# A hybrid transformer block in split fp32r: pair differences split by VectorE, attention weights as neighbour differences, and an earlier split of the first head

## The reference

```
h += 1/2 SwiGLU(RMSNorm(h));  h += StickBreaking(RMSNorm(h));  h += 1/2 SwiGLU(RMSNorm(h))
out = RMSNorm(h)[frames]
```

```
A[t,s] = sigmoid(z_ts) * prod_{s<j<t} (1 - sigmoid(z_tj)),   s < t,   z = q k / sqrt(128)
```

## Time and profile before

| | us |
|---|---|
| median of 3 runs | 2092.15 |
| profiled execution, and its span | 2091.31, 2089.4 |
| PE busy | 1978.4 (95%) |
| PE weight loads busy | 1795.3 (86%) |
| VectorE busy | 1115.4 (53%) |
| POOL busy | 986.9 (47%) |
| ScalarE busy | 684.7 (33%) |

### The profile page before, as it was taken

How to read it: one execution, slowest core, us unless ns; L and a number is a source line. 1 busy time by engine, 2 the same in 40 slices (tenths; PEclk the granted TensorE clock), 3 DMA queues, 4 the chain that set the end, 5 groups by cost and what they waited for, 6 DMA issues and landing times.

```text
span 2089.4 us, 35300 instructions
## 1 busy us (share of the span) xinstructions
PE 1978.4 (95%) x12868; PEld 1795.3 (86%) x12868; DVE 1115.4 (53%) x1587; ACT 684.7 (33%) x1227; POOL 986.9 (47%) x646
## 2 busy tenths in 40 slices
PE   7899999999999997999989999979999999899998
PEld 6899999999999987999978887767777777788886
DVE  5755554544555558333378870275444444454445
ACT  5322222222121233222289981242222222221112
POOL 4654545445444424444477762344454454543340
PEclk9999999999999998999999999989999999999999
DMA  3122222222323201333322112012222222233222
GB/s 123 49 77 87 66 86 71 80 91 103 122 81 102 80 21 51 111 97 106 102 83 71 61 51 61 21 30 66 85 66 84 84 72 85 86 132 115 80 91 81
DMA packets 165366, 167.74 MB, mean 80 GB/s; under 512 B 7984, under 2 KB 130864, under 8 KB 165312
## 3 DMA queue, kind: packets, MB, share of 16 engines
q1 hardware_dynamic: 165312, 166.99, 25.0%
HBM read 126.74 MB, written 40.22 MB: 80 GB/s over the span
## 4 chain that ended last, share of the span: by engine, by line
PE 46%; issue 27%; POOL 16%; ACT 5%; DVE 4%; DMA 1%; POOLq 0%; ACTq 0%; DVEq 0%; SPq 0%
PE psum L1366 15%; PE psum L1367 14%; PE psum L1368 14%; POOL arena L555 13%; PE psum L1393 2%; POOL arena L573 2%; ACT scratch L974 1%; ACT arena L939 1%; DVE scratch L1269 1%; DVE arena L1086 1%; DMA scratch<-w_out_dram 1%; ACT psum L976 1%; DVE psum L1059 0%; PE psum L1586 0%; DMA scratch<-w_o_dram 0%
## 5 line engine op out<-in xcount | busy, mean ns | idle before, releaser
L1366 PE MATMUL psum<-arena 128*128 128x260 f32 (+3 forms) x4028 | 1290.5, 320 | 73.9 <-issue 30.1
L1368 PE MATMUL psum<-arena 128*128 128x260 f32 (+3 forms) x4028 | 1268.9, 315 | 0.0
L1367 PE MATMUL psum<-arena 128*128 128x260 f32 (+3 forms) x4028 | 1267.4, 315 | 0.0
L1366 PEld LDWEIGHTS psum<-arena 128*128 128x128 f32 x4028 | 764.3, 190 | 142.7 <-issue 48.5
L1368 PEld LDWEIGHTS psum<-arena 128*128 128x128 f32 x4028 | 763.1, 189 | 47.1
L1367 PEld LDWEIGHTS psum<-arena 128*128 128x128 f32 x4028 | 763.3, 190 | 46.8 <-issue 3.6
L555 POOL TENSOR_TENSOR arena<-scratch,arena 128x512 fp32r<-128x512 f32 x365 | 509.1, 1417 | 551.7 <-ACT arena L754 551.7
L754 ACT ACTIVATE arena<-scratch 128x512 fp32r<-128x512 f32 x371 | 212.0, 622 | 492.8 <-DMA scratch<-w_in_dram 255.8
L1123 DVE SCALAR_TENSOR_TENSOR h<-psum,h 128x260 f32<-128x260 f32 (+1 forms) x496 | 249.7, 504 | 210.7 <-PE psum L1368 210.5
L1135 DVE TENSOR_TENSOR scratch<-scratch,psum 128x520 f32<-128x520 f32 (+1 forms) x265 | 182.6, 689 | 328.7 <-PE psum L1368 313.5
L1138 DVE TENSOR_TENSOR scratch<-scratch 128x512 f32<-128x512 f32 x200 | 235.6, 1178 | 220.6 <-POOL arena L555 196.3
(11 more groups left out here) (80 smaller groups left out, 1053.0 us busy)
## 6 DMA issues: line engine op xcount, KB each, us to landing
scratch<-w_in_dram SPq DMA_DIRECT2D x88, 512.0 KB, 4.9
scratch<-w_out_dram SPq DMA_DIRECT2D x22, 1024.0 KB, 4.9
qkv<-scratch SPq DMA_DIRECT2D x48, 260.0 KB, 2.1
scratch<-w_qkv_dram SPq DMA_DIRECT2D x24, 512.0 KB, 4.5
scratch<-qkv SPq DMA_DIRECT2D x24, 512.0 KB, 3.7
hidden<-scratch SPq DMA_DIRECT2D x44, 260.0 KB, 2.1
scratch<-hidden SPq DMA_DIRECT2D x11, 1040.0 KB, 4.9
hidden<-scratch SPq DMA_DIRECT2D x44, 256.0 KB, 2.1
```

The costliest lines, as they stand in the source:

```text
L1366: nc.tensor.matmul(dst, wh, xh, start=start, stop=False, skip_group_check=True)
L1367: nc.tensor.matmul(dst, wh, xl, start=False, stop=False, skip_group_check=True)
L1368: return nc.tensor.matmul(dst, wl, xh, start=False, stop=stop, skip_group_check=True)
```

## The change

1. **Homes.** B21 moves from xy and its three neighbours into the region of v1, beside B12 and T3, and v7 shares its region with v3 and no longer with v1. So `copy_x(0)` no longer waits for p_up 2, ScalarE's high parts of T3 wait for the six plain products that read v7, and its high parts of T2 wait for T4.
2. **Order.** The low parts of T1 (v2) go from POOL to VectorE. VectorE makes T1, T3, the first plain_up, the low parts of T1 and T3, and only then T2, T4 and the second plain_up. ScalarE does copy_x(0) before the high parts of T3. In FFN2 the rows of B21 are made after the last add of the output projection and their high parts after the last root.
3. **Attention.** One sigmoid of -z in place in PSUM replaces L974 and L976. POOL subtracts the row's neighbour. At the first step of each block (8 of 14) an extra one-column subtraction clears the row's first entry; at the others POOL also waits for its own previous step. The scan of a last step is one column longer.
4. **First head.** ScalarE's wait for the last QKV unit asks for its third product and no longer for its seventh; POOL splits k and q before it clears the rows.

The diff, cut:

```
-REGION_OF = ((0, 1, 2, 3, 4, 5, 6, 1), (4, 6, 0, 2, 5, 1, 3, 6), (0, 1, 3, 4, 2, 5, 6, 1))
+REGION_OF = ((0, 1, 2, 3, 4, 5, 6, 3), (4, 6, 0, 2, 5, 1, 3, 2), (0, 1, 3, 4, 2, 5, 6, 4))
-LO_BY_DVE = ((4, 6, 3, 1, 5), (6, 3, 1, 5), (6, 3, 1, 5))
-LO_BY_POOL = ((0, 7, 2), (0, 4, 7, 2), (0, 4, 7, 2))
+LO_BY_DVE = ((4, 6, 2, 3, 1, 5), (6, 2, 3, 1, 5), (6, 2, 3, 1, 5))
+LO_BY_POOL = ((0, 7), (0, 4, 7), (0, 4, 7))
...
-            if name == "B21":
-                return flat(n, (xy, c22, u0, scratch[:, 7752:])[k][:, 0:HALF[n]])
-            v, low = {"B12": (3, 1), "T3": (3, 1), "B22": (5, 0), "T2": (5, 0), "T4": (5, 1)}[name]
+            v, low = {"B21": (1, 0), "B12": (1, 1), "T3": (1, 1), "B22": (5, 0), "T2": (5, 0), "T4": (5, 1)}[name]
...
                     pool.wait_ge(left, S * hd + s + 1)
-                    nc.gpsimd.tensor_tensor(row, beta[s % 3][:, 0:n], row, ALU.mult).then_inc(weights, 1)
+                    if first_step(s):
+                        key = row[:, 0:1]
+                        nc.gpsimd.tensor_tensor(key, key, key, ALU.subtract)
+                        row, behind = row[:, 1:], behind[:, 1:]
+                    else:
+                        pool.wait_ge(weights, S * hd + s)
+                    nc.gpsimd.tensor_tensor(row, row, behind, ALU.subtract).then_inc(weights, 1)
...
+            for part_of in (("k", 0), ("k", 1), ("q", 0), ("q", 1)):
+                split(*part_of, 0, 0)
             pool.wait_ge(ffns[QKV]["w_lo"], PRODUCTS * UNITS[QKV])
             nc.gpsimd.memset(scratch[:, 0:21 * P], 0.0).then_inc(const_set, 1)
-            for part_of in (("k", 0), ("k", 1), ("q", 0), ("q", 1)):
-                split(*part_of, 0, 0)
...
                     product_over(u, 0)
-                    if isinstance(u, int) and u == 0:
-                        act.wait_ge(s["p_up"], 2)
-                    else:
-                        act.wait_ge(s["c12"], u)
+                    wait(act, s["c12"], u)
...
                     first_weight(1)
-                    split_rows(n, 3)
                     plain_gate(1)
                     first_weight(5)
                     first_weight(3)
+                    copy_x(0)
+                    split_rows(n, 3)
                     split_rows(n, 1)
-                    copy_x(0)
                     split_rows(n, 5)
...
-                    if not (first and before(s) < 0):
-                        act.wait_ge(weights, S * hd + before(s) + 1)
-                    nc.scalar.activation(beta[s % 3][:, 0:n], bank, ACT.Sigmoid, scale=Q_SCALE).then_inc(broken, 1)
-                    act.wait_ge(broken, S * hd + s + 1)
-                    nc.scalar.activation(bank, beta[s % 3][:, 0:n], ACT.Copy, scale=-1.0, bias=1.0).then_inc(kept, 1)
+                    nc.scalar.activation(bank, bank, ACT.Sigmoid, scale=-Q_SCALE).then_inc(kept, 1)
...
-            act.wait_ge(ffns[QKV]["used"], PRODUCTS * UNITS[QKV])
+            act.wait_ge(ffns[QKV]["used"], PRODUCTS * (UNITS[QKV] - 1) + 3)
...
                 combine(n, "T1", "B12", "B11", over_split=0)
                 combine(n, "T3", "B22", "B12", over_split=7)
+                plain_up(0)
+                rows_lo(n, 2)
+
+                dve.wait_ge(ffns[n]["w_lo"], 4)
+                rows_lo(n, 3)
                 combine(n, "T2", "B22", "T1", over_split=6)
                 combine(n, "T4", "B21", "T2")
-
-                dve.wait_ge(norms[n]["un"], STEPS_TO["T4"] + HK)
-                plain_up(0)
-                rows_lo(n, 3)
                 plain_up(1)
                 rows_lo(n, 1)
                 rows_lo(n, 5)
```

More of the change, by code:

```diff
@@ L204, in build @@
         plain_x = plain("plain_x", 6 * 1024, (META_TILE + 1) * D_MODEL)
-        plain_regions = {j: plain(f"plain{j}", 6 * 1024 + (PRODUCTS - 1 - j) * 4160, 4160) for j in range(1, 6)}
+        plain_regions = {j: plain(f"plain{j}", 6 * 1024 + (PRODUCTS - 1 - j) * 4160, 4160) for j in (1, 5, 6)}
         arena = sbuf("arena", [P, 35392], F32R)
@@ L269, in build @@
         rows = [scratch[:, at:at + tiles * P] for at, tiles in zip(ROW_AT, ROW_TILES)]
-        beta = [scratch[:, at:at + cols] for at, cols in zip(BETA_AT, (BANK, 400, 400))]
         raw_v = piece(scratch, 3592, TOKENS)
@@ L746, in norm_halves @@
                     root(c)
-                if n != FFN2:
-                    split_rows(n, 4)
+                split_rows(n, 4)
                 if n == FFN1:
@@ L803, in plain_gate @@
                     act.wait_ge(s["p_used"], 3 + 4 * c)
-                    if n == QKV and c == 1:
-                        act.wait_ge(norms[n]["un"], STEPS_TO["T4"] + HK)
                     out, bank = flat(n, (g0, (g1 if ffn else c22))[c][:, 0:half]), target(n, "ab"[c])
@@ L1083, in rows_lo @@
                 for k in range(HK):
+                    if v == 1:
+                        lo_made(dve, n, 3, k)
                     ins = inputs(n, v)
@@ L1311, in _ @@
                     rows(FFN2, "B11")
-                if n == KT + 5:
-                    rows(FFN2, "B21")
                 add_output(n)
+            rows(FFN2, "B21")
             reciprocal(FFN2, 1)
```

22 lines of the change are left out of this document (9 added, 13 removed).

## The result

The changed kernel takes **2050.56 us** (median of 4 runs, 2046.47 to 2053.36), beside 2091.18 us for the kernel before in the same comparison (2082.39 to 2094.78). The ratio is 0.9826, interval 0.980 to 0.9852. The forecast was 2061 us, its range 2049 to 2076. A repeat in a later comparison gave 2048.72 us beside 2079.31 for the kernel before: the changed kernel's time repeats, while the gain (40.6 us here, 30.6 there) moves with the kernel before. The experiments take that up.

The account below looks back on a forecast made before the run. PE was taken as bound by stops in the first units and before the first score, and by nearly full engines in the attention; 18.0 + 5.1 + 6.8 = 29.9 us off 2091.3 gave 2061 us, range 2049 to 2076.

Parts of the forecast that it names:

- What bounds the first units: Unit 0, three stages: copy_x(0), then the chain to plain_up stops PE; 4.5, 4.5, 4.7 us stops left, gain 18.0 us.
- The stops before were taken as constants: Unit 0: gain is stop before (6.86 us FFN1, 12.33 QKV, 12.51 FFN2) minus stops after, 18.0 us.
- The clock: First units: slow stretch expected behind the second stop as before; no change booked, upper end 5.6 us.
- T1's low parts at nothing: First units: four instructions moved to VectorE, 3.1 us, up to twice that beside POOL, costed at nothing.
- Into the attention: Before the first score: splits end earlier, PE starts near 1043.0 and not 1048.15, gain 5.1 us.
- The attention: Eight heads: ScalarE relieved of 6.3 us a head; 0.85 us a head gained, 6.8 in all, at most 11.0.
- The attention gives nothing: Rival, attention: PE waits for VectorE, as full as before; gain 23.1 us, 2068 us, chance 0.15.
- POOL is starved: First units rival: low parts wait behind VectorE, 4 to 12 us, or T2, T4 slowed, 13; 2073 us, chance 0.15.
- Slower: Rival, attention: POOL's extra instructions at 0.9 us each lengthen heads; 2115 us, break-even 0.69 us each, chance 0.03.
- All of it: Rival, whole kernel: clock doesn't fall and attention gets its 11.0 us; gain 41.7 us, 2050 us, chance 0.12.

Follow-up runs that it names:

- attention-alone kernel: The kernel before with only the change's attention (one sigmoid in place, POOL's subtraction, longer scan), units and entry as before: 2064.97 us, ratio 0.9925.

## Why the prediction came out as it did, step by step

- **What bounds the first units: right.** The copy and the chain to the second plain_up are where it put them. The first stops are 0.74, 0.74 and 0.73 us (0.8 expected), product 3 starts 9.8, 9.4 and 9.7 us behind product 0's end (10.2), and plain_up ends the second stop. The second stops are 3.06, 2.66 and 3.29 us, not 3.7, 3.7 and 3.9: T3's low parts take 2.45 us from start to start in QKV and not the 3.09 of the earlier trace rows, which were taken while POOL was at work on low parts of its own; here POOL was idle (its last one ended at 801.62). Products 4 and 2 take 6.0 us in FFN1 and QKV and not 5.7, and 5.7 in FFN2 and not 5.5. All stops together are 11.2 us against 13.7: 2.5 us of the miss.
- **The stops before were taken as constants: this is the step that was lucky.** The sum took 6.86, 12.33 and 12.51 us as what these stages cost. But each stage has one of two outcomes in a given run, 6.1 to 6.9 and 12.3 to 13.1. Three short ones would have made the gain some 12 us smaller, and the kernel before ranges from 2073.8 to 2094.8 us over all comparisons, where the changed one, whose second stops repeat within 0.1 us, stays within 2046.5 to 2053.4. The time itself fell at the edge of the range: 2050.56 us is 1.6 above its lower end, and the repeat, 2048.72, is below it.
- **The clock: half right, and that by chance.** In FFN1 and QKV it fell behind the second stop as forecast; behind the 3.29 us stop of FFN2 it stayed up, and there the slow stretch that the kernel before paid was spared. FFN2's stops account for 12.51 - 4.02 = 8.5 us of its 10.6. Windows of PE in the changed kernel (length, busy, granted clock), at 1.2 GHz in the first two and at 2.4 in the third:

```profile
77.00:78.00 1.00, 1.00 (x7) 0.50 0.59 181
811.00:812.00 1.00, 1.00 (x7) 0.50 0.78 258
1366.00:1367.00 1.00, 1.00 (x6) 1.00 0.71 225
```

  The forecast booked no change in any stage, with 5.6 us as the upper end; it was some 2 us. Another trace of the same kernel, of the repeat, has the same stops (3.07, 2.65 and 3.25 us) with other outcomes: the clock fell in FFN1, stayed up in QKV and fell in FFN2. Windows in QKV and FFN2 there:

```profile
809.00:810.00 1.00, 1.00 (x11) 1.00 0.60 147
1363.00:1364.00 1.00, 1.00 (x4) 0.50 0.47 114
```

  So the clock behind the second stop has two outcomes as well, and the sum had one of them.
- **T1's low parts at nothing: right, and narrowly.** They took 6.3 us beside POOL, the "up to twice" of the text, and ended at 800.5, as product 0 did (800.84). T3's low parts then wait for ScalarE, not for these. What the text did not see is that on POOL they would cost 7 us.
- **Into the attention: right for the splits, wrong for what is late next.** The first score comes 5.0 us earlier (5.1). The clearing "about when the first scan is due" stops PE for 1.15 us, and head 1's k, which no term had, for 2.34; the attention is 1.9 us longer for them than in the attention-alone kernel (188.2 and 186.3). SP's queue was not followed past the entry: load_k(1) stands behind load_v(0), which waits for the last store of the stage.
- **The attention: right mechanism, mis-sized.** 10.5 us with the start-up stops against 6.8. "Short of the whole because VectorE keeps its load" failed: VectorE keeps 21.05 us of 23.14 and PE hardly waits. The term looked at how full the engines are; that made 0.62 to 0.66 us a head, and the place of the second instruction, between a score and its scan, another 0.78. PE's idle time was no hard bound either: a head gained 1.4 us with 0.38 us of idle time left, and the attention alone 12.4 us, above the 11.0 that were called the most. ScalarE's load came to 16.49 us (15.9); POOL's to 16.56 and not 19.3, less than the 17.81 before, so the added column was cheap (0.19 us, 0.185 expected) and "POOL's subtraction reads and writes as the multiplication did" was on the dear side: 0.854 us for 400 columns, against 1.049 for the multiplication.
- **The rivals.** *The attention gives nothing* is excluded by the head of 23.14 us. *POOL is starved* did not happen: plain_up ends the second stops, and T2 and T4 take 2.52 us each. Of its two halves the first is turned round by the kernel before: a POOL that stands through VectorE's run is the good outcome there (6 to 7 us), a POOL that gets in between is the bad one (12 to 13 us). The second half, T2 and T4 slowed by POOL, is this bad one. *Slower* needed 0.69 us an instruction and had 0.19. *All of it* (2050 us, chance 0.12) is where the time came to lie, by another split: the attention's 12.4 us (attention alone) less 1.9 for its start-up stops, 2 of 5.6 us of clock, 2.5 us of shorter stops, and the 1.4 us of the rest.

The Trainium skill, SBUF — State Buffer, "Who interferes with whom", adds to its rule that issue order decides who blocks. The trace bears out that the two engines exclude each other: where VectorE's differences meet POOL's low parts, they take turns or one stands. That the order of issue decides which, it doesn't show: POOL begins 1.44 us behind T1 in both outcomes. And POOL's instruction stood not for one instruction of VectorE but through a whole run of them, 9.58 us where one by itself takes 1.3.

## What to carry to other kernels

A stop that another engine's timing makes can have more than one length: compare the same stretch in the other stages and in a second trace before its length goes into a sum, and read a wide spread of run times as a hint of two outcomes. Where two engines run nearly full in a written order, count the instructions between a result and its consumer as well as the load; here a copy off that way cost half of what it cost in it. And when a wait is taken away, follow every queue, the transfers' too, one step past it: what was hidden behind the old wait (a clearing, a load) is the next stop, and here changes of order alone got 11 to 13 us more (by medians of different comparisons).

## What the runs showed of the hardware

- VectorE's differences with two SBUF inputs and POOL's subtractions shared the time in two patterns in the same code: 1.7 us for a pair in turns (VectorE 7 us for four), or VectorE at 2.52 us for four and one instruction of POOL standing for 9.58 us until the run was over.
- The clock fell behind stops of 3.06 and 2.66 us (FFN1, QKV) and not behind one of 3.29 us (FFN2), in the same trace. In the repeat it stayed up behind 2.65 us (QKV) and fell behind 3.25 us (FFN2). The length of a stop alone did not decide it.
- The same ScalarE copy of about 0.45 us, 14 a head, cost a head 0.62 to 0.66 us when nothing waited for it and 1.4 us between a score and its scan.
- A one-column subtraction on POOL took 192 to 206 ns. A subtraction of a row from itself, one column on, took less than the multiplication of the row by another buffer: of the kernel before and of the changed one, by line and form,

```profile
L661 POOL TENSOR_TENSOR scratch<-scratch 128x400 f32<-128x400 f32 x32 | 33.6, 1049 | 8.4 <-DVE scratch L1269 7.2
```

```profile
L663 POOL TENSOR_TENSOR scratch<-scratch 128x400 f32<-128x400 f32 x24 | 20.5, 854 | 7.5 <-DVE scratch L1264 7.5
```

  Whether the operation, the buffers or VectorE's scans beside it make the difference was not tried.
